# Three modulation vectors moved from TensorE's attention loop to VectorE, gates one job later

## The chip, the cores and the metric

The kernel runs on one core of a Trainium2 chip. It is one launch with a hand-written instruction stream for each engine: TensorE (PE, with PEld for its weight loads), VectorE (DVE), ScalarE (ACT), GpSimd (POOL) and SyncE (SP), which issues nearly all DMAs. The metric is the device time of one execution in microseconds; lower is better. The median of three runs before the change is 1446.85 us (1446.82 to 1449.01).

## The reference, cut to what matters

One layer of a hybrid diffusion block on 1024 latent tokens and 256 context tokens of 1024 features, all in float32. What the change touches is the modulation: six vectors of 1024 features made from one conditioning vector.

```python
def modulation(cond, w, b):            # w is ada_w, 1024 x 6144
    m = jax.nn.silu(cond) @ w + b
    return jnp.split(m, 6, axis=-1)
# h  = rmsnorm(x, g_mix_pre) * (1 + scale_1) + shift_1        vectors 1 and 0
# x1 = x + gate_1 * rmsnorm(mixer(h) @ w_out, g_mix_post)     vector 2
# h2 = rmsnorm(x1, g_ffn_pre) * (1 + scale_2) + shift_2       vectors 4 and 3
# y  = x1 + gate_2 * rmsnorm(swiglu(h2), g_ffn_post)          vector 5
```

The mixer is an input projection (1024 to 2816), then three groups of channels side by side: a long convolution by transforms, neighbourhood attention with 8 heads plus all context keys, and a gated linear recurrence (RG-LRU) that runs forward and backward. Then come the output projection, and a SwiGLU feed-forward of width 2816.

## The kernel before, in words

Features lie on partitions, tokens along the free dimension. A large float32 product is made of three passes: each weight tile and each input is split into a rounded head (`w_hi`, by ACT) and a rest (`w_lo`, by POOL), and TensorE sums head x head, head x rest and rest x head. One unit of this is called a job: 24 matmuls of up to 512 columns (`product` L1917 and following, `lat_job` L2078). The heads and rests of a job's weights are made while the job before it runs, from a double-buffered `raw` that SP loads (`raw_dma`, issue at L490; it waits until the rest of the weights two jobs back is made, since that frees the buffer).

The order on each engine is the order in which the code is written; semaphores tie the engines together. The stages are:

- Start (0 to about 114 us): filter tables, spectra, and modulation vectors 0 and 1 by TensorE (`mod_sums` L2017, `mod_columns` L2025, 16 column matmuls with the row of sums as the stationary tile).
- Input projection: 54 jobs (`JOBS`), from 114 to 445 us. The outputs are moved out of PSUM by DVE for even jobs and ACT for odd ones up to job 19 (`lat_out`), by ACT afterwards. Between jobs, TensorE runs the gates of the recurrence (`lru_gates` L2099; `GATES_AFTER` puts gates 0 to 3 behind jobs 6, 7, 11, 13), then transposes and transforms of the convolution. DVE does the short convolutions and scans of the recurrence (table `after`: behind job j it runs `after[j]`), then the convolution's stages. Gates 0 need `lru_conv(0)`, which DVE runs behind job 4.
- Attention: 32 units (4 head pairs x 8 blocks of queries), 453 to 606 us. TensorE's loop in step n is scores(n), turn(n-1), values(n-2). DVE adds the bias table and takes the minimum (L1723), ACT takes the exponential (L998), DVE normalises (L1733), TensorE transposes the probabilities (L2231, L2239), ACT copies them (L1010, L1012), TensorE multiplies by the values (L2254), and DVE copies the result (L1737). POOL makes the bias tables of the next head pair (L1211) and the rests of its keys (L1194). ACT makes the heads of the next keys in step 2 of each eight (`key_heads` L931).
- In each turn TensorE also makes one of the 32 chunks (128 features) of modulation vectors 2 to 5: 8 float32 matmuls with the conditioning vector as stationary tile (L2234, 16 instructions, since a float32 matmul is two), whose weights SP brought as `ada1` (512 KB per chunk); ACT copies the row of sums (L1011), and a matmul of one column in values() turns it into a column (L2248, two instructions).
- Output projection, then the feed-forward in two halves of 512 tokens: 22 tiles of two jobs (gate and up, `gu_tile`), and 24 down jobs. In a tile, DVE combines the two products (L1825, L1828) and makes the rest of the result (L1832); in tiles 5 to 12 of the first half DVE adds the mixer's residual behind it (L1773 and following). Tiles 13 to 21 hold nothing more.
- The end: the last down job, its square on ACT (L1105), the sum over features, a root, and four output rows of blocks written out.

## Time and profile before

| what | us |
|---|---|
| median of three runs | 1446.85 |
| the profiled execution | 1447.58 |
| its span, first to last instruction | 1445.8 |
| PE busy | 1403.6 (97%) |
| DVE busy | 744.8 (52%) |
| ACT busy | 552.8 (38%) |
| POOL busy | 612.9 (42%) |

The busy shares are means over stages with different limits, so a stage has to be read by itself: by the chain of work that ended last, by what an engine waited for in a stretch, and by the timeline of a few microseconds. Matmuls are pipelined, so a row's duration is longer than the distance to the next; distances are taken from start to start.

### The profile page before, as it was taken

Reading aid. Unit: us, or ns where it says so; the run is one execution under the profiler, and the core shown is the slowest. Engines: PE = TensorE matmul, PEld = TensorE weight load, DVE = VectorE, ACT = ScalarE, POOL = GpSimd, SP = SyncE. Lnnn points to the kernel's source line nnn. Section 1 sums busy time; section 2 is a strip of 40 time slices with the busy share of each in tenths; the row PEclk is TensorE's granted clock in tenths of the full one; section 3 lists DMA queues with packets and bytes.
Section 4 is the critical chain, followed back from the end, with each engine's and each line's share of the span. In section 5 each row is a group of like instructions: output and inputs, shape, how many; then the busy total and the mean of one; then the engine's idle time right before and its main releaser. Section 6 shows DMA issues by size and latency. Waiting matters only on the chain.

```text
span 1445.8 us, 20378 instructions
## 1 busy us (share of the span) xinstructions
PE 1403.6 (97%) x7745; PEld 1148.6 (79%) x7745; DVE 744.8 (52%) x1024; ACT 552.8 (38%) x863; POOL 612.9 (42%) x291
## 2 busy tenths in 40 slices
PE   5999999999998999999999999999999999999997
PEld 1589667899987888888788888888888888888885
DVE  7764557893945887447755541145456411110122
ACT  5662544321314777643432323332232223233222
POOL 3353122061435554383444444444444444444442
PEclk9999999999999999999999999999999999999999
DMA  9852111414213455443233333333333433332332
GB/s 328 319 168 70 48 44 29 131 30 131 59 30 101 137 139 151 147 143 105 74 101 88 94 98 99 94 95 99 94 98 97 136 102 101 94 95 85 94 100 85
DMA packets 236450, 156.67 MB, mean 108 GB/s; under 512 B 10531, under 2 KB 221873, under 8 KB 236251
## 3 DMA queue, kind: packets, MB, share of 16 engines
q1 hardware_dynamic: 234387, 148.70, 34.1%
q10 hardware_dynamic: 1992, 6.99, 1.3%
q8 instruction: 48, 0.79, 0.2%
q14 instruction: 23, 0.19, 0.0%
HBM read 147.25 MB, written 8.81 MB: 108 GB/s over the span
## 4 chain that ended last, share of the span: by engine, by line
PE 88%; DVE 5%; ACT 3%; issue 1%; DVEq 0%
PE ps L1923 36%; PE ps L1928 18%; PE ps L2091 11%; PE ps L2096 5%; PE ps L2254 2%; PE ps L2231 2%; PE ps L2192 2%; PE ps L2109 1%; PE ps L2150 1%; PE ps L2138 1%; PE ps L1985 1%; PE ps L1972 1%; PE ps L2234 1%; PE ps L1992 1%; ACT pr L998 1%
## 5 line engine op out<-in xcount | busy, mean ns | idle before, releaser
L1130 POOL TENSOR_TENSOR w_lo<-raw,w_hi 128x1024 fp32r<-128x1024 f32 x152 | 375.9, 2473 | 439.3 <-ACT w_hi L708 439.3
L1923 PE MATMUL ps<-hb_hi,w_hi 128*128 128x512 f32 x768 | 300.7, 392 | 1.6 <-DVE hb_lo L1790 1.6
L1923 PE MATMUL ps<-hb_lo,w_hi 128*128 128x512 f32 x768 | 298.9, 389 | 0.0
L708 ACT ACTIVATE w_hi<-raw 128x1024 fp32r<-128x1024 f32 x152 | 160.1, 1053 | 169.6 <-PE ps L1928 164.6
L1928 PE MATMUL ps<-hb_hi,w_lo 128*128 128x512 f32 x768 | 191.1, 391 | 0.0
L1150 POOL TENSOR_TENSOR w_lo<-raw,w_hi 128x1024 fp32r<-128x1024 f32 x21 | 88.6, 4219 | 222.2 <-ACT w_hi L862 222.2
L1923 PEld LDWEIGHTS ps<-hb_hi,w_hi 128*128 128x128 f32 x768 | 144.2, 188 | 33.2 <-DVE hb_lo L1790 3.4
L1928 PEld LDWEIGHTS ps<-hb_hi,w_lo 128*128 128x128 f32 x768 | 144.2, 188 | 31.2 <-issue 1.4
L1923 PEld LDWEIGHTS ps<-hb_lo,w_hi 128*128 128x128 f32 x768 | 144.2, 188 | 29.7 <-issue 0.2
L2091 PE MATMUL ps<-ha_hi,w_hi 128*128 128x512 f32 (+2 forms) x432 | 163.7, 379 | 3.1 <-ACT p_hy L869 2.8
L2091 PE MATMUL ps<-ha_lo,w_hi 128*128 128x512 f32 (+2 forms) x432 | 161.3, 373 | 0.0
L1923 PE MATMUL ps<-a_hi,w_hi 128*128 128x512 f32 x352 | 138.3, 393 | 0.0
L1923 PE MATMUL ps<-a_lo,w_hi 128*128 128x512 f32 x352 | 137.1, 389 | 0.0
L1828 DVE SCALAR_TENSOR_TENSOR a_f<-g_t,ps 128x512 f32<-128x512 f32 x44 | 30.2, 687 | 166.9 <-PE ps L1928 166.9
L1078 ACT ACTIVATE a_hi<-a_f 128x512 f32 (+1 forms) x44 | 27.8, 632 | 204.8 <-DVEq L1830 204.8
L2096 PE MATMUL ps<-ha_hi,w_lo 128*128 128x512 f32 (+2 forms) x432 | 99.1, 371 | 0.0
L2091 PEld LDWEIGHTS ps<-ha_hi,w_hi 128*128 128x128 f32 x432 | 81.7, 189 | 17.4 <-issue 3.2
L2091 PEld LDWEIGHTS ps<-ha_lo,w_hi 128*128 128x128 f32 x432 | 81.7, 189 | 10.4
L2096 PEld LDWEIGHTS ps<-ha_hi,w_lo 128*128 128x128 f32 x432 | 80.0, 188 | 10.3
L1928 PE MATMUL ps<-a_hi,w_lo 128*128 128x512 f32 x352 | 87.6, 389 | 0.0
L1825 DVE SCALAR_TENSOR_TENSOR g_t<-g_t,ps 128x512 f32<-128x512 f32 x44 | 30.2, 687 | 94.5 <-ACT g_t L1074 93.1
L1923 PEld LDWEIGHTS ps<-a_hi,w_hi 128*128 128x128 f32 x352 | 66.1, 188 | 13.8 <-issue 0.2
(293 smaller groups left out, 2104.6 us busy)
## 6 DMA issues: line engine op xcount, KB each, us to landing
raw<-in_ffn_w_gu SPq DMA_DIRECT2D x88, 512.0 KB, 3.8
ada1x<-in_ada_w SPq DMA_DIRECT2D x32, 512.0 KB, 4.0
raw<-in_ffn_w_down SPq DMA_DIRECT2D x32, 512.0 KB, 3.8
raw<-in_w_in SPq DMA_DIRECT2D x22, 512.0 KB, 3.9
ada<-in_ada_w SPq DMA_DIRECT2D x4, 2048.0 KB, 21.9
raw<-in_w_out SPq DMA_DIRECT2D x16, 512.0 KB, 3.9
raw<-in_ffn_w_down SPq DMA_DIRECT2D x16, 384.0 KB, 3.4
raw<-in_ktab SPq DMA_DIRECT2D x8, 512.0 KB, 5.5
```

Of the source, the lines that this page charges most:

```text
L708: act.activation(w_hi[:, b, :], raw[:, b, :], ACT.Copy).then_inc(hi_done, 1)
L1130: pool.tensor_tensor(w_lo[:, b, :], raw[:, b, :], w_hi[:, b, :].bitcast(F32), ALU.subtract).then_inc(lo_done, 1)
L1150: pool.tensor_tensor(w_lo[:, b, :], raw[:, b, :], w_hi[:, b, :].bitcast(F32), ALU.subtract).then_inc(llo, 1)
L1825: dve.scalar_tensor_tensor(g_t[:], g_t[:], 1.0, ps[:, 0, :], ALU.add, ALU.mult).then_inc(acc_free, 1)
L1828: dve.scalar_tensor_tensor(a_f[:], g_t[:], 0.5, ps[:, 1, :], ALU.mult, ALU.mult).then_inc(acc_free, 1)
L1923: pe.matmul(dst, w_hi[:, b, k * P:(k + 1) * P], x, start=start and i_ == 0 and n == 0, stop=False)
L1928: ins = pe.matmul(dst, w_lo[:, b, k * P:(k + 1) * P], rhs(k)[0], start=False, stop=stop and k == nk - 1)
L2091: pe.matmul(dst, w_hi[:, b, k * P:(k + 1) * P], x[:, k, a:z], start=k == 0 and n == 0, stop=False)
L2096: ins = pe.matmul(dst, w_lo[:, b, k * P:(k + 1) * P], ha_hi[:, k, a:z], start=False, stop=k == KT - 1)
L2192: ins = pe.matmul(dst, q_[hh, 4 * rb + cb, :], rhs, start=i == 0, stop=i == 2)
L2231: pe.transpose(ps[0:m, 4 + e, c * P:(c + 1) * P], pr[:, b, e, a:a + m], ident[:])
L2254: ins = pe.matmul(ps[hh, 7, 0:P], vtm[0:m, hp, tile, hh], pT[0:m, b, e, c, :], start=c == 0, stop=c == 4)
```

## The change

Modulation vectors 2 and 3 are made by DVE in the input projection. SP brings rows of `ada_w` in eight transfers of 1 MB, each holding two k-tiles of one vector (`rows_dma`; contiguous pieces of 4 KB), and DVE multiplies each k-tile by the conditioning value of its partition and adds it up (`modulation_rows`, two operations of 128x1024 per transfer). TensorE then sums over partitions with 16 matmuls of one column ahead of job 18, and DVE adds the bias (`modulation_columns`). Vector 5 is made in the same way in the first half of the feed-forward, one k-tile behind each of tiles 13 to 20, with eight transfers of 512 KB and 8 matmuls behind the last tile. Attention keeps the eight chunks of vector 4, in its last eight units. Gates 0 and 1 go behind jobs 7 and 8. At the end, the last square goes to the sum without DVE's addition, the last transposes stand behind the sum, and a square root of two numbers is put ahead of the second half's down jobs.

```diff
-GATES_AFTER = {6: 0, 7: 1, 11: 2, 13: 3}
+GATES_AFTER = {7: 0, 8: 1, 11: 2, 13: 3}
+ADA_UNIT = 24
+        adq = [p_hy[:, 2 * r:2 * r + 2, :] for r in range(2)]
+        adq_sum = [p_hy[:, 4 + v, :] for v in range(2)]
 # SP, input projection
+            def rows_dma(q):
+                if q >= 2:
+                    sp.wait_ge(mod_rd, 16 + q - 1)
+                else:
+                    sp.wait_ge(kjob, 8)
+                c, m = 2 * (q % 4), 2 + q // 4
+                sp.dma_start(adq[q % 2], ada[:, c:c + 2, m * D:(m + 1) * D]).then_inc(ada_ld[q % 2], 16)
+            rows_dma(0)
+            rows_dma(1)
             # (the 16 loads of l_w)
-            for fi in range(2, 4):
-                lat_raw(fi)
+            rows_dma(2)
+            rows_dma(3)
+            lat_raw(2)
+            lat_raw(3)
+            rows_dma(4)
+            rows_dma(5)
+            lat_raw(4)
+            lat_raw(5)
+            rows_dma(6)
+            rows_dma(7)
             sp.wait_ge(rz_ld, 16)
             sp.dma_start(rpad[:, 4:19, 8:39], A["na_rpb"][0]).then_inc(rp_ld, 16)
+            lat_raw(6)
+            lat_raw(7)
             # (the 16 issues of rskew)
-            for fi in range(4, 10):
-                lat_raw(fi)
+            lat_raw(8)
+            lat_raw(9)
 # SP, attention
-                chunk_dma(n)
+                if n >= ADA_UNIT + 2:
+                    chunk_dma(n - ADA_UNIT)
 # SP, feed-forward, first half (in place of the loop over tiles)
+                    def gate_rows(c):
+                        if c >= 2:
+                            sp.wait_ge(mod_rd, 32 + c - 1)
+                        else:
+                            sp.wait_ge(job_done, J_FFN)
+                        sp.dma_start(adf[c % 2][:], ada[:, c, 5 * D:6 * D]).then_inc(ada_ld[c % 2], 16)
+                    for i in range(1, FT):
+                        for b in range(2):
+                            raw_dma(b, J0 + 2 * i + b, src_g(i, b))
+                        if i == 5:
+                            gate_rows(0)
+                            gate_rows(1)
+                        if 14 <= i < 20:
+                            gate_rows(i - 12)
 # ACT
-                    act.activation(arow1[:, u % 2, :], ps[:, 6, 256:384], ACT.Copy)
+                    if u >= ADA_UNIT:
+                        act.activation(arow1[:, u % 2, :], ps[:, 6, 256:384], ACT.Copy)
+                    act.activation(arec[:, 0, :], ones[:, 0:2], ACT.Sqrt)     # ahead of the second half's down jobs
 # DVE
+            def modulation_rows(q):
+                dve.wait_ge(ada_ld[q % 2], 16 * (q // 2 + 1))
+                acc = adq_sum[q // 4]
+                for r in range(2):
+                    c = 2 * (q % 4) + r
+                    if c == 0:
+                        link(dve.tensor_scalar(acc, adq[q % 2][:, r, :], sil[:, 0, 0:1], None, ALU.mult))
+                    else:
+                        link(dve.scalar_tensor_tensor(acc, adq[q % 2][:, r, :], sil[:, 0, c:c + 1], acc, ALU.mult, ALU.add))
+                dve.nop().then_inc(mod_rd, 1)
+            def modulation_columns():
+                dve.wait_ge(mod_done, 19)
+                link(dve.tensor_tensor(mod[:, 16:32, 0], ps[:, 7, 0:16], colA[:, 64:80], ALU.add))
-            after = {4: lambda: lru_conv(0), 6: lambda: lru_conv(1),
+            after = {0: lambda: (modulation_rows(0), modulation_rows(1)), 2: lambda: (modulation_rows(2), modulation_rows(3)),
+                     4: lambda: lru_conv(0), 6: lambda: (lru_conv(1), *map(modulation_rows, range(4, 8))),
-                     18: lambda: (lru_input(3, 9), lru_backward(3), lru_join(3, 10)),
+                     18: lambda: (modulation_columns(), lru_input(3, 9), lru_backward(3), lru_join(3, 10)),
+                    for c in range(KT):                                       # feed-forward, first half
+                        gu_tile(13 + c)
+                        dve.wait_ge(ada_ld[c % 2], 16 * (c // 2 + 9))
+                        # tensor_scalar for c == 0, else scalar_tensor_tensor into adf_sum, as above
+                        dve.nop().then_inc(mod_rd, 1)
 # PE
+                if j == 18:
+                    pe.wait_ge(l_gate, 24)
+                    pe.wait_ge(mod_rd, 24)
+                    for m in range(2 * KT):
+                        ins = pe.matmul(ps[:, 7, m:m + 1], adq_sum[m // KT][:, (m % KT) * P:(m % KT + 1) * P], ones[:, 0:1],
+                                        start=True, stop=True)
+                    ins.then_inc(mod_done, 1)
+                if u >= ADA_UNIT:            # turn(u): the eight matmuls of a chunk; values(v): its column
+                    pe.wait_ge(ada_ld[b], 16 * ((u - ADA_UNIT) // 2 + 5))
 # (first half of the feed-forward, behind the last tile: 8 such column matmuls of adf_sum)
 # the end
-                    down_columns(KT - 1)
             pe.wait_ge(n_sum, 6)
-            for q in range(4):
-                ins = pe.matmul(ps[:, 0, q:q + 1], nrm[:, q * P:(q + 1) * P], ones[:, 0:1], start=True, stop=True)
+            for half in range(2):
+                for last in range(2):
+                    if last and half == 0:
+                        pe.wait_ge(y_sq, KT)
+                    for q in (2 * half, 2 * half + 1):
+                        src = sq[:, (KT - 1) % 2, q * P:(q + 1) * P] if last else nrm[:, q * P:(q + 1) * P]
+                        ins = pe.matmul(ps[:, q % 2, q // 2:q // 2 + 1], src, ones[:, 0:1], start=not last, stop=last == 1)
             ins.then_inc(n_ps, 1)
+            down_columns(KT - 1)
```

## Rows read from the trace of the kernel before

**Rows 1.** the page: the chain that ended last, shares by engine.

```profile
PE 88%; DVE 5%; ACT 3%; issue 1%; DVEq 0%
```

**Rows 2.** timeline of one attention turn, TensorE's weight loads (start, us, instructions).

```profile
524.62 0.86 PEld L2231 LDWEIGHTS ps<-ident,pr 128*128 128x128 f32 x8 [0.19 <-issue]
...
525.65 0.38 PEld L2234 LDWEIGHTS ps<-ada1x,silp 128*32 128x32 f32 x16 [0.17 <-issue]
526.22 0.20 PEld L2239 LDWEIGHTS ps<-ident,pr 128*128 128x128 f32 x2 [0.20 <-issue]
526.39 0.30 PEld L2248 LDWEIGHTS ps<-selc,arow 128*128 128x128 f32 x2
526.71 1.07 PEld L2254 LDWEIGHTS ps<-pT,vtm 96*64 96x64 f32 x20
...
529.02 0.86 PEld L2231 LDWEIGHTS ps<-ident,pr 128*128 128x128 f32 x8 [0.19 <-issue]
```

**Rows 3.** waits between engines from 483 to 570 us (total us, times, longest).

```profile
DVE pr L1723 <- PE ps L2192: 5.5, 11, 0.8
```

**Rows 4.** timeline of DVE and POOL in the same turns.

```profile
523.18 0.55 DVE L1733 TENSOR_SCALAR pr<-pr,arec 128x640 f32<-128x640 f32 x1
...
524.74 0.82 DVE L1723 CUSTOM_DVE_ANT_0 pr<-ps,tb 128x640 f32<-128x640 f32 x1 [0.78 <-PE ps L2192]
...
526.39 2.63 POOL L1211 TENSOR_TENSOR tb<-gt,mask 128x384 f32<-128x384 f32 x2 [5.84 <-DVE amin L1723]
...
526.76 1.18 DVE L1733 TENSOR_SCALAR pr<-pr,arec 128x640 f32<-128x640 f32 x1
...
529.49 0.81 DVE L1723 CUSTOM_DVE_ANT_0 pr<-ps,tb 128x640 f32<-128x640 f32 x1
```

**Rows 5.** timeline of DVE in the turn with the key heads.

```profile
509.42 0.17 DVE L1732 RECIPROCAL arec<-asum 128x1 f32<-128x1 f32 x1 [1.41 <-ACT pr L998]
```

**Rows 6.** timeline of TensorE: first gates, first channel transposes.

```profile
149.88 4.51 PE L2109 MATMUL ps<-l_u,l_w 64*64 64x256 f32 x24 [1.51 <-DVEq L1477]
...
256.53 1.12 PE L2122 MATMUL ps<-ident,conv 128*128 128x128 f32 x8 [1.57 <-DVEq L1528]
```

**Rows 7.** timeline of TensorE's weight loads at the start's column matmuls.

```profile
67.65 1.98 PEld L2025 LDWEIGHTS ps<-selc,arow 128*128 128x128 f32 x16
```

**Rows 8.** timeline of DVE and SP in the input projection; a transfer's row.

```profile
138.76 0.56 DVE L1461 TENSOR_SCALAR p_kv<-ps 128x384 f32<-128x384 f32 x1 [8.50 <-PE ps L2096]
...
170.23 0.69 DVE L1461 TENSOR_SCALAR p_xg<-ps 128x512 f32<-128x512 f32 x1 [13.72 <-PE ps L2096]
...
214.13 1.22 DVE L1514 SCALAR_TENSOR_TENSOR l_q<-l_q,p_xg 128x1024 f32<-128x1024 f32 x1
...
130.27 1.21 SPq L516 DMA_DIRECT2D raw<-in_w_in  x2
...
ada<-in_ada_w SPq DMA_DIRECT2D x4, 2048.0 KB, 21.9
```

**Rows 9.** the feed-forward: chain of TensorE, then DVE, POOL, SP, ACT.

```profile
845.29 3.63 PE ps L1923 x16
...
847.78 0.75 DVE L1773 SCALAR_TENSOR_TENSOR a_f<-yo,gmix,rstd 128x512 f32<-128x512 f32 x1 [0.16 <-DVE a_lo L1832]
...
847.92 2.87 POOL L1130 TENSOR_TENSOR w_lo<-raw,w_hi 128x1024 fp32r<-128x1024 f32 x1 [4.02 <-ACT w_hi L708]
...
1135.25 1.69 SPq L490 DMA_DIRECT2D raw<-in_ffn_w_gu  x2
...
1140.36 1.06 ACT L708 ACTIVATE w_hi<-raw 128x1024 fp32r<-128x1024 f32 x1 [2.53 <-DMA raw<-in_ffn_w_gu]
```

**Rows 10.** timeline of the end.

```profile
1434.44 0.69 DVE L1894 TENSOR_TENSOR nrm<-nrm,sq 128x512 f32<-128x512 f32 x1 [11.92 <-ACT sq L1105]
...
1435.43 0.97 PEld L2423 LDWEIGHTS ps<-ones,nrm 128*128 128x128 f32 x8
...
1436.52 0.16 DVE L1902 TENSOR_SCALAR var<-ps 128x4 f32<-128x4 f32 x1 [1.39 <-PE ps L2423]
```

More of the change, by code:

```diff
@@ L271, in program @@
         hb3_lo = at("hb3_lo", P_KV + 32768, [KT, HALF], F32R)
+        adf = [at("adf0", S_ + 32768, [D]), at("adf1", S_ + 36864, [D])]
+        adf_sum = at("adf_sum", S_ + 40960, [D])
         ysq = at("ysq", S_ + 2048, [HALF])
@@ L634, in chunk_dma @@
             def chunk_dma(n):
-                ada_dma(ada1, n % 2, 16 + n - 1 if n >= 2 else None, ada[:, :, (16 + n) * P:(17 + n) * P], ada_ld)
+                ada_dma(ada1, n % 2, 24 + n - 1 if n >= 2 else None, ada[:, :, (32 + n) * P:(33 + n) * P], ada_ld)
             sp.wait_ge(rs_ld, 256)
@@ L656, in _ @@
             sp.wait_ge(pv_done, 32)
-            sp.wait_ge(mod_done, 50)
+            sp.wait_ge(mod_done, 18 + 1 + 32 - ADA_UNIT)
             for q in range(4):
@@ L674, in _ @@
                 if h == 0:
-                    phase(J0, FT, src_g)
+                    def gate_rows(c):
[12 more added lines that the diff above has]
+                            gate_rows(i - 12)
                 else:
@@ L1740, in _ @@
             dve.tensor_tensor(hm_lo[5][:], mix_src(5, 0), hm_hi[5][:].bitcast(F32), ALU.subtract).then_inc(m_ld, 1)
-            dve.wait_ge(mod_done, 50)
-            link(dve.tensor_tensor(mod[:, 16:48, 0], ps[:, 7, 384:416], colA[:, 64:96], ALU.add))
+            dve.wait_ge(mod_done, 18 + 1 + 32 - ADA_UNIT)
+            link(dve.tensor_tensor(mod[:, 32:40, 0], ps[:, 7, 384 + ADA_UNIT:416], colA[:, 80:88], ALU.add))
             dve.nop().then_inc(modp, 1)
             link(dve.tensor_tensor(gmix[:], mod[:, 16:24, 0], colA[:, 24:32], ALU.mult))
-            link(dve.tensor_tensor(gffn[:], mod[:, 40:48, 0], colA[:, 40:48], ALU.mult))
             link(dve.scalar_tensor_tensor(affn[:], mod[:, 32:40, 0], 1.0, colA[:, 32:40], ALU.add, ALU.mult))
@@ L1858, in _ @@
                     dve.nop().then_inc(n_sum, 1)
+                    for c in range(KT):
+                        gu_tile(13 + c)
+                        dve.wait_ge(ada_ld[c % 2], 16 * (c // 2 + 9))
+                        if c == 0:
+                            link(dve.tensor_scalar(adf_sum[:], adf[0][:], sil[:, 0, 0:1], None, ALU.mult))
+                        else:
+                            link(dve.scalar_tensor_tensor(adf_sum[:], adf[c % 2][:], sil[:, 0, c:c + 1], adf_sum[:], ALU.mult, ALU.add))
+                        dve.nop().then_inc(mod_rd, 1)
                 else:
@@ L1875, in _ @@
                                         ps[:, 4 + 2 * (q % 2):6 + 2 * (q % 2), :].rearrange("p a b -> p (a b)")).then_inc(o_ev, 1)
-                i0 = 7 if h else 13
+                i0 = 7 if h else 21
                 with dve.Fori(i0, FT) as i:
@@ L1882, in _ @@
                 if h == 0:
+                    dve.wait_ge(mod_done, 28)
+                    link(dve.tensor_tensor(mod[:, 40:48, 0], ps[:, 7, 0:8], colA[:, 88:96], ALU.add))
+                    link(dve.tensor_tensor(gffn[:], mod[:, 40:48, 0], colA[:, 40:48], ALU.mult))
                     rstd_of(3)
@@ L1891, in _ @@
                 else:
-                    for k in range(1, KT):
+                    for k in range(1, KT - 1):
                         dve.wait_ge(y_sq, k + 1)
@@ L1901, in _ @@
             dve.wait_ge(n_ps, 6)
-            dve.tensor_scalar(var4[:], ps[:, 0, 0:4], 1.0 / D, EPS, ALU.mult, ALU.add).then_inc(n_var, 1)
+            dve.tensor_scalar(var4[:].rearrange("p (c b) -> p b c", b=2), ps[:, 0:2, 0:2], 1.0 / D, EPS, ALU.mult, ALU.add).then_inc(n_var, 1)
             for b in range(2):
@@ L1907, in _ @@
             link(dve.reciprocal(rstd4[:], var4[:]))
+            dve.wait_ge(t_tp, 4 + KT)
             for q in range(4):
@@ L2166, in _ @@
                     inverse(o, part, V_ROWS[o])
+                if j == 18:
[5 more added lines that the diff above has]
+                    ins.then_inc(mod_done, 1)
                 lat_job(j, (lambda: turn_channels(1)) if j == 22 else None)
                 if j in GATES_AFTER:
-                    if j == 6:
+                    if j == 7:
                         pe.wait_ge(lw_ld, 256)
@@ L2231, in turn @@
                         pe.transpose(ps[0:m, 4 + e, c * P:(c + 1) * P], pr[:, b, e, a:a + m], ident[:])
-                pe.wait_ge(ada_ld[b], 16 * (u // 2 + 1))
-                for k in range(KT):
-                    ins = pe.matmul(ps[32 * (k % 4):32 * (k % 4) + 32, 6, 256:384], silp[:, k, :],
-                                    ada1[:, b, k * P:(k + 1) * P], start=k < 4, stop=k >= 4)
-                ins.then_inc(mod_rd, 1)
+                if u >= ADA_UNIT:
+                    pe.wait_ge(ada_ld[b], 16 * ((u - ADA_UNIT) // 2 + 5))
+                    for k in range(KT):
+                        ins = pe.matmul(ps[32 * (k % 4):32 * (k % 4) + 32, 6, 256:384], silp[:, k, :],
+                                        ada1[:, b, k * P:(k + 1) * P], start=k < 4, stop=k >= 4)
+                    ins.then_inc(mod_rd, 1)
                 a, m = chunks[4]
@@ L2247, in values @@
                     pe.wait_ge(ot_free, v)
-                pe.matmul(ps[:, 7, 384 + v:385 + v], arow1[:, b, :], selc[:, 0:1], start=True, stop=True).then_inc(mod_done, 1)
+                if v >= ADA_UNIT:
+                    pe.matmul(ps[:, 7, 384 + v:385 + v], arow1[:, b, :], selc[:, 0:1], start=True, stop=True).then_inc(mod_done, 1)
                 for c in range(5):
@@ L2373, in _ @@
                 if h == 0:
+                    pe.wait_ge(mod_rd, 40)
+                    for m in range(KT):
+                        ins = pe.matmul(ps[:, 7, m:m + 1], adf_sum[:, m * P:(m + 1) * P], ones[:, 0:1], start=True, stop=True)
+                    ins.then_inc(mod_done, 1)
                     sum_over_features(3, nrm)
```

## Prediction

> **What bounds the kernel now.** Start with the chain that ended last: 88% of it is TensorE [rows 1], so an instruction taken from TensorE is worth its distance, unless another engine sets the pace at that place. The removed work lies in attention, so read one turn there next. From one turn's transposes to the next turn's it is 529.02 - 524.62 = 4.40 us [rows 2]. Of these, the chunk takes 526.22 - 525.65 = 0.57 us and its column 526.71 - 526.39 = 0.32 us: 0.89 us per turn. TensorE alone would so give 24 x 0.89 = 21.4 us. But is TensorE what each turn waits for? The waits of the stretch with the 20 steps 6 to 25 say how long DVE's first operation of a step waited for the scores: 5.5 us, in 11 of the 20 [rows 3]. The other nine started without a wait. DVE and POOL show why: normalising takes 0.55 us where POOL is idle and 1.18 us under POOL's bias table; after that one, the next step of DVE starts at 529.49 with no wait in front of it, 4.75 us after the last, while the step before had 0.78 us to spare [rows 4]. So in this stretch DVE, slowed by POOL, is nearly as late as TensorE. What TensorE saves comes back only up to DVE's waits.
>
> **Attention, what is removed.** In steps 6 to 25 the gain is the 5.5 us that DVE waited [rows 3]. Steps 0 to 5 overlap POOL throughout; I give them nothing. In the step with the key heads DVE waits 1.41 us for ACT [rows 5], and ACT loses one small copy there; in three such steps I take 0.5 us for the three together (it lies between 0 and their 4.2 us of waits, and the copy is the smallest of what ACT does there). Steps 26 to 31 keep their chunks and gain nothing. Sum: -6.0 us. Ends: 0 us if DVE and ACT set every step and the 5.5 us reappear elsewhere, -21.4 us if TensorE set every step. I stay at 6.0, since a wait is a ceiling for what its releaser can give. After the change TensorE should need 4.40 - 0.89 = 3.51 us for a step and DVE without POOL 4.40 - 0.78 = 3.62 us, so DVE is the later one in all of them.
>
> **Gates one job later.** Today TensorE waits 1.51 us for the short convolution ahead of the first gates [rows 6]. A job lies between afterwards, 24 matmuls at 3.63/16 us = 5.4 us [rows 9], so the wait goes: -1.5 us. What comes later instead is gates 0 on ACT and the recurrence behind them; DVE next needs them behind job 8, where it idles 13.72 us [rows 8]. Ends: -1.5 and +1 us.
>
> **What DVE does instead.** An operation of 128x1024 with two inputs in SBUF takes 1.22 us [rows 8]. Four of them behind job 0 (about 5 us) and four behind job 2 stand against idle stretches of 8.50 us at job 4, and one like it at job 2; eight behind job 6 (10 us with the gaps) stand against 13.72 us [rows 8]. They come free in time if their transfers do. Transfers 0 and 1 are issued as soon as the last spectrum is stored, while DVE is busy with other work. Transfers 2 and 3 (2 MB) are issued behind the 16 small loads of the gates' weights, and the raw weights of job 6 now stand behind them in SP's queue. Four transfers of 2 MB in flight together took 21.9 us [rows 8], 2.7 us per MB, so 2 MB delay the weights by at most 5.5 us. Today they are issued at 130.27 [rows 8]; with 0.7 us for two more issues, 5.5 us and the 5.1 us that weights took behind another transfer [rows 9], they land at 141.6 at the latest. Job 6 ends at 149.88 - 1.51 = 148.4 today and so starts at 143.0; ACT's head takes 1.06 us [rows 9] and must begin by 141.9. I take 0 us, with 3 us as the other end. Transfers 6 and 7 wait for DVE's own progress, land some 4 us later, and push the eight operations to about 13 us, near the whole idle stretch; a POOL operation in the way adds 2.4 us. TensorE needs the bank that DVE frees behind them only when gates 1 (4.51 us) and job 9 (5.4 us) are done, 10 us after job 8. I take 0, with +3 us as the other end.
>
> **Columns.** The 16 matmuls of one column ahead of job 18 are 32 instructions. At the start, 16 such instructions took 1.98 us of weight loads [rows 7], at the end 8 took 0.97 [rows 10]: 0.12 us each, 3.8 us. Nothing hides them, since TensorE waits for no one at job 18, and the chain of DVE that it waits for later (1.57 us at the first channel transposes [rows 6]) begins behind job 18 and moves with it. DVE's bias addition stands ahead of that chain: +0.2 us. The eight in the feed-forward are 16 instructions: +1.9 us. Ends for all: 4 to 7 us.
>
> **The feed-forward's first half.** DVE is idle most of a tile, so the one operation behind each of tiles 13 to 20 costs it nothing. The queue to watch is SP's. From tile 14 to 19, SP waits for DVE's operation behind the tile before, and the raw weights of the next tile's first job stand behind this wait. Count from job start 845.29, which is the end of a tile [rows 9]. Work like DVE's new operation starts at 847.78 today, 0.14 us ahead of POOL, and is not slowed; POOL is (2.87 us) [rows 9]. The new one, of 1.22 us, ends at 849.0, and SP goes on at about 849.3: the row transfer, then the raw weights at about 849.7. Elsewhere in this trace SP issued weights right behind another transfer at 1135.25, and ACT could start on them at 1140.36, 5.1 us later [rows 9]. So ACT starts at 854.8 and is done at 855.9; the job that needs them starts two jobs after 845.29, at 856.2. The slack is 0.3 us: I take 0, and name the rest as a rival.
>
> **The end.** Today DVE's last addition (from 1434.44) and the wait of the sum behind four transposes put the variance at 1436.52 [rows 10]. Afterwards 12 of the 16 small instructions follow the square, which is ready at about 1434.4: 12 x 0.12 = 1.45 us, so variance at about 1436.0: -0.5 us (ends 0 and -0.8). The square root put ahead costs ACT time where it has a job in hand: 0.
>
> **Sum.** -6.0 - 1.5 + 0 + 3.8 + 0.2 + 1.9 + 0 - 0.5 = -2.1 us. The profiled execution took 1447.58 us (span 1445.8 and 1.8 around it) and would take 1445.5; it stands 0.7 us above the median of 1446.85, so the median comes to 1444.8 us.
>
> **Rivals.**
> - *SP's queue in the feed-forward* (slower). The 0.3 us of slack are used up if POOL takes its turn first: then DVE's operation ends near 850.8 + 1.2 = 852.0 rather than 849.0, ACT has the weights 3.0 us later, and TensorE waits 2.7 us in each of six tiles: +16 us, 1461 us. If SP or the transfer is only 1 us slower than counted it is 6 x 0.7 = +4 us, 1449 us. It decides from 0.3 us of delay on. For it: the 0.14 us between DVE and POOL. Against it: in the row shown DVE came first, with the same instructions ahead of it.
>   The Trainium skill, page "SBUF — State Buffer", section "SBUF: two separate sides", says that a DVE operation with two SBUF inputs and a GpSimd operation that reads SBUF hold their port in turn, and that the one that starts second fully blocks. The trace agrees as to order: POOL, starting second, took 2.87 us. By that rule this rival is all or nothing per tile.
> - *TensorE's pace in attention* (faster). POOL's tables start when DVE has finished with the old ones; if shorter turns let more of them fall beside operations that aren't slowed, the nine unwaited steps shorten too. Each slow pair costs 2 x (1.18 - 0.55) = 1.3 us [rows 4]; half of nine gone is 6 us more: 1439 us. Against it: the table starts at 526.39 because DVE finished its minimum just before, so they stay tied.
> - *The projection's queue* (slower). Row transfers land late, DVE is still on them when job 8's or job 4's bank should come free, or job 6's weights come late: +3 to +6 us, 1448 to 1451 us. For it: 0.3 us of room for the weights of job 6 by the upper bound.
> - *Attention gives nothing*: DVE's waits were only reordered, and the columns' 5.9 us stay: 1446.85 - 1.5 + 5.9 - 0.5, 1450.7 us. For it: nine of 20 steps of DVE wait for nothing. Against: 11 do.
>
> **Chances.** 0.2% of the time is 2.9 us, what a measurement can tell from no change: faster is below 1444.0, slower above 1449.7. Forecast 0.50 (own range 1442.5 to 1447; 0.13 of it below 1444.0). TensorE's pace 0.18, all faster. SP's queue 0.15 (0.10 slower, 0.05 within). Projection's queue 0.10 (0.05 slower). Attention gives nothing 0.07 (0.05 slower). Together faster 0.31, same 0.49, slower 0.20. The range for 8 in 10 is 1440 to 1450.5.
>
> **What would show it.** Attention: starts of L1723 in steps 6 to 25 without waits for scores, and the same steps about 5.5 us shorter together; L1733 still near 1.2 us under L1211. No wait ahead of the first L2109. The weight loads ahead of job 18 within 4 us. L708 in tiles 15 to 20 starting at most 0.3 us before it would make L1923 wait; a wait of L1923 for `w_hi` there shows the first rival. No new wait of L2091 for `lfree` or `w_hi` from job 4 to job 10. The prediction is wrong if attention shortens by less than 3 or more than 9 us, or if TensorE gains a wait over 1 us anywhere else.

## The result, and the profile after

| | us |
|---|---|
| kernel before, median of 4 runs beside it | 1447.93 (1446.82 to 1449.02) |
| changed kernel, median of 4 runs | 1459.47 (1459.03 to 1459.72) |
| ratio, 95% interval | 1.008, 1.0068 to 1.0091 |
| profiled execution, span before and after | 1445.8 and 1457.6 |

The change makes the kernel 11.5 us slower. Forecast were 1444.8 us and a range up to 1450.5 us. The forecast failed in one place above all, and a table by stage finds it. Each line is the start of the same instruction in both traces, subtracted; the first column says what the prediction had for the stage.

| stage | predicted | measured |
|---|---|---|
| start to job 6 of the projections | 0 | -0.9 |
| job 6 to job 17 (gates one job later) | -1.5 | -1.2 |
| job 17 to the start of job 18 (16 columns) | +3.8 | +3.8 |
| job 18 to job 22 (bias added by DVE, and more) | +0.2 | +2.9 |
| rest of the projections | 0 | 0.0 |
| attention up to the output projection | -6.0 | -6.0 |
| output projection, feed-forward to tile 15 | 0 | 0.0 |
| tiles 15 to 21 of the feed-forward's first half | 0 | +12.0 |
| tile 21 to the first down job (8 columns) | +1.9 | +1.8 |
| the end | -0.5 | -0.5 |

The sum of the measured column is +11.9, the two spans differ by 11.85. The first line is no effect of the change: among the ten profiled executions below job 0 starts anywhere from 111.2 to 115.5 us, also in kernels that differ only much later. All comparisons by trace are therefore made over distances inside a run. In this table they run between starts of TensorE's matmuls.

Start with the page of the changed kernel, its chain by engine, which answers to [rows 1]: TensorE's share fell from 88% to 77%, and DMA and SP's queue stand in it for the first time.

```profile
PE 77%; DVE 10%; ACT 4%; issue 2%; DMA 2%; SPq 1%; DVEq 0%; ACTq 0%
```

Next, who waits between 860 and 940 us (engine line waited for: us in total, times, longest):

```profile
ACT w_hi L751 <- DMA raw<-in_ffn_w_gu: 28.6, 6, 6.0
...
PE ps L1996 <- ACT w_hi L751: 7.4, 5, 2.4
```

TensorE waits for the rounded weights, ACT for the raw ones. The timeline from the first row operation to the first late matmul, five engines in order of time (start, us, engine, instructions, in brackets the idle time ahead); tile 15 starts at 865.53:

```profile
857.30 0.75 DVE L1925 TENSOR_SCALAR adf_sum<-adf,sil 128x1024 f32<-128x1024 f32 x1
857.45 2.86 POOL L1175 TENSOR_TENSOR w_lo<-raw,w_hi 128x1024 fp32r<-128x1024 f32 x1 [4.02 <-ACT w_hi L751]
...
858.14 0.34 SPq L709 DMA_DIRECT2D adf<-in_ada_w  x1
858.52 2.18 SPq L495 DMA_DIRECT2D raw<-in_ffn_w_gu  x2
...
864.10 1.06 ACT L751 ACTIVATE w_hi<-raw 128x1024 fp32r<-128x1024 f32 x1 [3.22 <-DMA raw<-in_ffn_w_gu]
...
865.24 2.40 POOL L1175 TENSOR_TENSOR w_lo<-raw,w_hi 128x1024 fp32r<-128x1024 f32 x1 [4.93 <-ACT w_hi L751]
...
865.53 0.39 PE L1996 MATMUL ps<-hb_hi,w_hi 128*128 128x512 f32 x1
...
867.34 0.86 DVE L1894 TENSOR_TENSOR a_lo<-a_f,a_hi 128x512 fp32r<-128x512 f32 x1 [0.85 <-ACT a_hi L1122]
...
868.34 2.40 POOL L1175 TENSOR_TENSOR w_lo<-raw,w_hi 128x1024 fp32r<-128x1024 f32 x1 [0.69 <-ACT w_hi L751]
868.35 3.47 DVE L1927 SCALAR_TENSOR_TENSOR adf_sum<-adf,sil,adf_sum 128x1024 f32<-128x1024 f32 x1 [0.16 <-DVE a_lo L1894]
...
871.90 0.34 SPq L709 DMA_DIRECT2D adf<-in_ada_w  x1
872.29 1.06 SPq L495 DMA_DIRECT2D raw<-in_ffn_w_gu  x2
...
877.47 1.06 ACT L751 ACTIVATE w_hi<-raw 128x1024 fp32r<-128x1024 f32 x1 [5.71 <-DMA raw<-in_ffn_w_gu]
...
878.67 0.47 PE L1996 MATMUL ps<-hb_hi,w_hi 128*128 128x512 f32 x1 [2.11 <-ACT w_hi L751]
```

Read it from the top. At the first row operation DVE is 0.15 us ahead of POOL, as in [rows 9], and ends at 858.05; SP goes on, and the raw weights it issues at 858.52 reach ACT at 864.10, 5.6 us later, not the 5.1 us counted. That is in time for TensorE, but ACT has stood 3.2 us for them, so POOL's operation starts at 865.24, 0.3 us ahead of tile 15, instead of 3.6 us ahead of it. It still runs when DVE starts the operation ahead of the row operation (L1894, two SBUF inputs), which takes 0.86 us instead of 0.69 us. So the row operation starts 2.82 us behind the tile's start instead of 2.67 us, and POOL's next operation, which stands where it always did, 2.81 us behind the tile's start, is 0.01 us ahead of it. The row operation is held: it takes 3.47 us, 2.2 us more than the 1.28 us that it takes undisturbed, and ends 1.1 us behind POOL's. SP waits for it, the weights are issued at 872.29, and TensorE stands for 2.1 us. From the next tile on the late weights bring POOL 0.7 to 0.8 us ahead of the row operation, and each tile repeats it: five tiles, +2.3, +2.7, +2.2, +2.6 and +2.1 us.

In two of the five TensorE hardly stands (0.3 and 0.2 us) and works at a lower clock instead; these slices lie in tiles 17 and 19 (start and end, length, busy time of TensorE, of its weight loads, of DVE, ACT and POOL, then the granted clock, 1.00 being full speed, and two values of the DMA engines):

```profile
890.00:894.00 4.00, 1.76 (x4) 1.49 (x5) 1.99 (x2) 2.64 (x3) 1.82 (x1) 0.77 0.48 117
894.00:898.00 4.00, 4.00 (x15) 3.16 (x14) 3.84 (x2) 0.00 (x0) 3.37 (x2) 0.80 0.00 0
918.00:922.00 4.00, 3.21 (x9) 2.57 (x10) 2.65 (x2) 2.22 (x3) 3.28 (x2) 0.68 0.07 18
```

The clock is not what makes them long: there too the next tile's first matmul starts 0.14 us behind the end of ACT's head, as it does at 877.47 + 1.06 + 0.14 = 878.67, so the weights set the time.

The other unforeseen size stands behind the columns. TensorE's weight loads there, then the mean granted clock in slices of 4 us (the third value from the end of a line):

```profile
230.39 4.42 PEld L2244 LDWEIGHTS ps<-ones,p_hy 128*128 128x128 f32 x32
234.69 0.33 PEld L2164 LDWEIGHTS ps<-ha_hi,w_hi 128*128 128x128 f32 x1
...
235.34 0.33 PEld L2164 LDWEIGHTS ps<-ha_hi,w_hi 128*128 128x128 f32 x1
235.76 0.33 PEld L2164 LDWEIGHTS ps<-ha_lo,w_hi 128*128 128x128 f32 x1
```

```profile
226.00:230.00 4.00, 4.00 (x18) 3.27 (x17) 3.97 (x2) 0.98 (x1) 2.37 (x1) 0.93 0.08 20
230.00:234.00 4.00, 4.00 (x33) 3.88 (x31) 1.05 (x1) 1.54 (x2) 1.57 (x1) 0.92 0.39 115
234.00:238.00 4.00, 4.00 (x13) 3.32 (x13) 0.00 (x0) 0.00 (x0) 0.79 (x1) 0.50 0.44 128
238.00:242.00 4.00, 4.00 (x15) 3.19 (x14) 0.00 (x0) 0.00 (x0) 0.00 (x0) 0.72 0.01 3
```

From the first of the 32 loads to the first of job 18 it is 4.3 us; job 17 is 0.3 us shorter than before, so the stage is 3.8 us longer by the starts of the matmuls, as foreseen. But behind them the clock is at its lower level, 1.2 GHz: loads of job 18 stand 0.42 us apart instead of 0.23 us, though no row shows TensorE idle. That is most of the +2.9 us; 0.2 us of them are the bias addition.

The gates start without a wait where [rows 6] had 1.51 us, here TensorE's row:

```profile
152.80 4.51 PE L2182 MATMUL ps<-l_u,l_w 64*64 64x256 f32 x24
```

With the gates alone this makes job 6 to job 10 1.6 us shorter. Here it gives less, 1.2 us to job 17: from job 9 to job 11 TensorE takes 0.4 us more than in that kernel, and job 10 starts behind a wait of 0.15 us for DVE's move out of PSUM (L1506). Of the nine traced kernels with DVE's row operations in the projections six have this delay and three do not; what decides it was not looked into.

In attention, 483 to 570 us as in [rows 3], the waits of DVE for scores are gone, and one of TensorE for ACT is there instead, 10.3 us in total where the kernel before had 1.5 us:

```profile
PE ps L2311 <- ACT pT L1056: 10.3, 15, 1.4
```

And at the end the variance starts 2.2 us behind the last product instead of 2.7 us [rows 10]; here DVE's row:

```profile
1448.38 0.16 DVE L1974 TENSOR_SCALAR var<-ps 128x4 f32<-128x4 f32 x1 [13.48 <-PE ps L2513]
```

### The profile page after: what moved, and what is told of

Same layout as the page of the kernel before. It is cut to its first block, busy times and chain, and to the rows that moved or that the text cites. A ratio compares the mean times of both kernels' runs of the same rounds, so it can differ in the third digit from the quotient of the medians.

```text
span 1457.6 us, 19409 instructions
## 1 busy us (share of the span) xinstructions
PE 1398.7 (96%) x7369; PEld 1144.1 (78%) x7369; DVE 799.2 (55%) x1049; ACT 549.5 (38%) x840; POOL 615.7 (42%) x291
## 4 chain that ended last, share of the span: by engine, by line
PE 77%; DVE 10%; ACT 4%; issue 2%; DMA 2%; SPq 1%; DVEq 0%; ACTq 0%
PE ps L1996 34%; PE ps L2001 17%; PE ps L2164 9%; PE ps L2169 4%; ACT pr L1041 2%; DMA raw<-in_ffn_w_gu 1%; DVE pr L1796 1%; DVE pr L1786 1%; PE ps L2223 1%; PE ps L2211 1%; PE ps L2058 1%; DVE p_hy L1733 1%; PE ps L2045 1%; DVE adf_sum L1927 1%; PE ps L2065 1%
## 5 line engine op out<-in xcount | busy, mean ns | idle before, releaser
L1118 ACT ACTIVATE g_t<-ps 128x512 f32<-128x512 f32 x44 | 26.3, 598 | 136.3 <-PE ps L2001 136.3
```

Of the source, the lines that this page charges most:

```text
L1118: act.activation(g_t[:], ps[:, 0, :], ACT.Tanh, scale=0.5).then_inc(g_tanh, 1)
```

## The experiments

Ten kernels in three groups; each group has its own runs of the kernel before, and the ratios are against those.

| kernel | us, median | before beside it | ratio, 95% interval |
|---|---|---|---|
| rows one tile later | 1447.74 | 1447.24 | 1.0001, 0.9988 to 1.0014 |
| the same, columns ahead of job 17 | 1444.96 | 1447.24 | 0.9981, 0.9969 to 0.9993 |
| the same, columns spread | 1441.94 | 1447.24 | 0.9959, 0.9943 to 0.9975 |
| projections' part only | 1446.95 | 1447.24 | 0.9997, 0.9986 to 1.0008 |
| row operation with one input | 1456.90 | 1447.65 | 1.0054, 1.0041 to 1.0067 |
| row operation on half the columns | 1455.97 | 1447.65 | 1.0039, 1.0020 to 1.0058 |
| 16 columns alone | 1454.66 | 1447.65 | 1.0045, 1.0032 to 1.0057 |
| gates alone | 1447.22 | 1447.65 | 0.9997, 0.9988 to 1.0005 |
| row operation with its sum in PSUM | 1449.79 | 1447.31 | 1.0011, 0.9998 to 1.0024 |
| rows one tile later, operation in two parts | 1447.31 | 1447.31 | 0.9997, 0.9988 to 1.0006 |

### Rows one tile later

```
-                        if 14 <= i < 20:
-                            gate_rows(i - 12)
+                        if 15 <= i < 21:
+                            gate_rows(i - 13)
```

> Only the order in SP's queue changes: the row transfers 2 to 7 of the feed-forward stand one tile later (tiles 15 to 20), so SP waits for an operation of DVE that was done a tile before; the transfers, DVE's operations and their tiles are the same. Theory A (the wait in SP's queue holds back the raw weights of the next tile): the five tiles that took 2.4 us each too long lose it, -12 us against the changed kernel, 1447.5 us, and no wait of TensorE over 1 us for w_hi between tiles 14 and 20. Rival B (the six transfers of 512 KB themselves slow the weights): they still run beside the weights, so most of the 12 us stays, 1457 to 1459.5 us. Rival C (DVE's operation blocked by POOL, 3.2 to 3.5 us rather than 1.22 us, delays DVE's own work): it is still there, so 1457 to 1459.5 us.

The six row transfers are the same, but they are issued 3.0 us or more ahead of the next weights, not 0.4 us.

Measured: 1447.74 us, 11.7 us less than the changed kernel. In its trace tiles 15 to 21 take exactly as long as before the change (the difference to the kernel before stays at -4.56 us from tile 5 to tile 21). DVE and POOL of one tile:

```profile
864.13 0.69 DVE L1894 TENSOR_TENSOR a_lo<-a_f,a_hi 128x512 fp32r<-128x512 f32 x1 [0.84 <-ACT a_hi L1122]
864.99 1.28 DVE L1927 SCALAR_TENSOR_TENSOR adf_sum<-adf,sil,adf_sum 128x1024 f32<-128x1024 f32 x1 [0.16 <-DVE a_lo L1894]
...
865.13 3.40 POOL L1175 TENSOR_TENSOR w_lo<-raw,w_hi 128x1024 fp32r<-128x1024 f32 x1 [4.03 <-ACT w_hi L751]
```

All seven two-input row operations take 1.28 us, and POOL, coming 0.14 us later, takes 3.40 us. So the same operations and as many transfers cost nothing once SP's wait is one tile older: theory A. B is settled only as far as the transfers stand in this order; the kernel with the sum in PSUM, further down, keeps each right ahead of the weights and bounds it. C is not tested here, since DVE isn't held at all.

### How much is the hold, how much the way from SP to ACT

Three kernels leave every wait and transfer of the changed kernel in place and alter only DVE's row operation in the feed-forward. Each leaves something out of the gate vector, so their results are not the layer's: the running sum, half of the columns, or the true sum (what happens to be in PSUM is read in its place).

```
# cut: ".." stands for arguments left out
-  scalar_tensor_tensor(adf_sum[:], adf[c % 2][:], sil[..], adf_sum[:], ALU.mult, ALU.add)
+  tensor_scalar(adf_sum[:], adf[c % 2][:], sil[..], None, ALU.mult)          # one input
+  scalar_tensor_tensor(adf_sum[:, 0:HALF], adf[c % 2][:, 0:HALF], ..)        # half the columns
+  scalar_tensor_tensor(adf_sum[:], adf[c % 2][:], sil[..], ps[:, 4:6, :], ..)  # sum from PSUM
```

> The changed kernel as it is, with SP's waits in their places, but DVE's row operation of the feed-forward has one input in SBUF (a row times its scalar, nothing added, so the gate vector is wrong): 0.75 us instead of 1.28 us. Theory P (a DVE operation with two SBUF inputs that starts 0.01 us behind POOL is held until POOL is done, and that 2.2 us is what TensorE waits in each tile): with one input DVE isn't held, the operation stays at 0.75 us though POOL is in the same place, and at least 10 of the 12 us go: 1447.5 us. Rival L (the way from SP's issue to ACT, 5.6 us rather than the 5.1 us counted, is what makes each tile late, and the port only adds DVE time that nobody waits for): the operation ends 0.5 us earlier only, so at most 0.5 us a tile goes, 1456 to 1457 us.

> The changed kernel as it is, but DVE's row operations behind tiles 14 to 20 work on 512 of the 1024 columns (the gate vector is wrong in the other half): two inputs in SBUF, about 0.7 us, as short as the operation with one input. Theory P: it is held behind POOL like the full one whenever POOL starts first, 2.4 + 0.7 = 3.1 us instead of 3.47 us, so TensorE still waits some 2 us a tile: 1456 to 1457.5 us. Rival L (length of the operation, not the port): like the operation with one input, whatever that gives; if that one loses the 12 us, so does this one, 1447.5 us.

> The changed kernel as it is, all waits and transfers in their places, but the running sum that DVE's row operation adds to is read from PSUM instead of SBUF (so the gate vector is wrong): one SBUF input, no mode of double rate, about 1.3 us as before. DVE's operations of 128x512 with a PSUM input stayed at 0.69 us under POOL in the changed kernel's trace, so this one should not be held. Theory P (the hold behind POOL is what keeps TensorE waiting 2.4 us in each tile): 10 to 12 us go, 1447.5 to 1449.5 us, with at most 0.5 us a tile left of the way from SP to ACT. Rival L (that way alone, 5.6 us, makes the tiles late): the operation's length and SP's order are unchanged, so 1457 to 1459.5 us.

Measured with one input: 1456.90 us. Theory P's number is missed and L's is met, but the trace says why, and it isn't L's reason. POOL, then DVE:

```profile
869.27 2.39 POOL L1175 TENSOR_TENSOR w_lo<-raw,w_hi 128x1024 fp32r<-128x1024 f32 x1 [0.66 <-ACT w_hi L751]
...
869.31 2.90 DVE L1927 TENSOR_SCALAR adf_sum<-adf,sil 128x1024 f32<-128x1024 f32 x1
```

The operation with one SBUF input is held too: 2.90 us instead of 0.75 us, and tiles 15 to 21 still lose 9.2 us. What I had wrong was which operations are held, not whether the hold matters. The rows of before had shown it: L1733, a TENSOR_SCALAR with one tensor input, took 0.55 us with POOL idle and 1.18 us beside it [rows 4]. The Trainium skill, page "SBUF — State Buffer", section "SBUF: two separate sides", names a DVE operation in a mode that uses two ports beside the one with two SBUF inputs. The run agrees with it as far as it goes: this form does 1024 columns in 0.75 us where the one with two inputs takes 1.28 us, which looks like such a mode, and it was held for 2.15 us. The number of inputs alone does not explain the shorter time: with its second input in PSUM the operation takes 1.28 us as well (below).

Measured with half the columns: 1455.97 us, 0.03 us under P's range; held, 2.95 us instead of 0.75 us, and tiles 15 to 21 lose 9.4 us. Here are POOL and DVE:

```profile
868.04 2.40 POOL L1175 TENSOR_TENSOR w_lo<-raw,w_hi 128x1024 fp32r<-128x1024 f32 x1 [0.70 <-ACT w_hi L751]
...
868.04 2.95 DVE L1927 SCALAR_TENSOR_TENSOR adf_sum<-adf,sil,adf_sum 128x512 f32<-128x512 f32 x1 [0.16 <-DVE a_lo L1894]
```

Its twelve runs lie between 1444.78 and 1459.01 us, wider than any other's. Two of them are as fast as a kernel without the stall and three more lie near 1451 us; whether the chain of late tiles started later or not at all in those is not known, since the one execution with a trace (1457.23 us) has it.

Measured with the sum in PSUM: 1449.79 us, 0.3 us above P's range and 7.2 us below L's. The timeline has the same order as the changed kernel, POOL first by 0.03 us, but DVE's operation is not held:

```profile
870.52 2.40 POOL L1175 TENSOR_TENSOR w_lo<-raw,w_hi 128x1024 fp32r<-128x1024 f32 x1 [0.68 <-ACT w_hi L751]
...
870.55 1.28 DVE L1927 SCALAR_TENSOR_TENSOR adf_sum<-adf,sil,ps 128x1024 f32<-128x1024 f32 x1 [0.16 <-DVE a_lo L1894]
...
872.30 1.06 SPq L495 DMA_DIRECT2D raw<-in_ffn_w_gu  x2
...
877.62 1.06 ACT L751 ACTIVATE w_hi<-raw 128x1024 fp32r<-128x1024 f32 x1 [3.67 <-DMA raw<-in_ffn_w_gu]
...
890.41 0.47 PE L1997 MATMUL ps<-hb_hi,w_hi 128*128 128x512 f32 x1 [0.46 <-ACT w_hi L751]
```

Length, waits and transfers are those of the changed kernel, and tiles 15 to 21 cost 2.4 us instead of 12.0 us (0.1 to 0.7 us a tile). So 9.6 us of the 12.0 us are the hold of the row operation, shown by taking it away.

The 2.4 us that stay are in part the way over SP to ACT: from SP's issue it takes 5.1 to 5.7 us in these tiles, where the count had 5.1 us. Another part is a hold again: L1894, ahead of the row operation, takes 0.87 us in tile 15 and 1.3 to 1.7 us in the next five instead of 0.69 us, so the row operation starts 2.8 to 3.05 us behind the tile's start instead of 2.67 us. How much is each was not measured. The 2.4 us are also the most that the six transfers can cost by themselves.

And there was no slack for either. The count took 845.29 as the tile's start, which is a time of the chain; the matmul itself starts earlier, and the next tile's starts 10.88 us later, at 856.00. Here is TensorE's row of the kernel before:

```profile
845.12 0.39 PE L1923 MATMUL ps<-hb_hi,w_hi 128*128 128x512 f32 x1
```

In each late tile the first matmul starts 0.14 us behind the end of ACT's head. The count's 855.9 and 0.14 us make 856.0: the slack was nil, not 0.3 us.

### A hold that nobody waits for

```
+  for a, z in ((0, 256), (256, D)):      # on top of "rows one tile later"
+      scalar_tensor_tensor(adf_sum[:, a:z], adf[c % 2][:, a:z], .., adf_sum[:, a:z], ..)
```

> The kernel with the rows one tile later, and DVE's row operation in two parts of 256 and 768 columns, so that POOL, which was 0.14 us behind, gets its turn between them and the second part is held. The result is the same. Theory A (a held DVE operation costs only through what waits for it, and SP no longer waits for this one in the same tile): the second part takes 3 us or more and the time stays 1447.5 us. Rival C (the hold itself makes DVE's own work late): the second part ends before DVE's next operation is due in both cases by 0.3 us or less, so up to 1 us a tile, 1450 to 1453 us.

Measured: 1447.31 us. DVE's two parts together and POOL's operation that gets in between:

```profile
864.82 3.55 DVE L1928 SCALAR_TENSOR_TENSOR adf_sum<-adf,sil,adf_sum 128x256 f32<-128x256 f32 x2 [0.16 <-DVE a_lo L1894]
...
864.97 2.59 POOL L1175 TENSOR_TENSOR w_lo<-raw,w_hi 128x1024 fp32r<-128x1024 f32 x1 [4.03 <-ACT w_hi L751]
...
868.52 0.69 DVE L1887 SCALAR_TENSOR_TENSOR g_t<-g_t,ps 128x512 f32<-128x512 f32 x1 [0.15 <-ACT g_t L1118]
```

The hold is there in each of the seven tiles: the second part takes 3.03 us. DVE's next operation (L1887) starts 0.09 us later behind the tile's start than in the kernel without the split (6.36 and 6.27 us), and the tiles take as long as before the change. The hold by itself costs nothing (theory A); it costs only through SP's queue.

### The columns

16 matmuls of one column alone, added to the kernel before ahead of job 18:

```
+  if j == 18:
+      pe.wait_ge(l_gate, 24)
+      for m in range(2 * KT):
+          pe.matmul(ps[:, 7, m:m + 1], ident[:], ones[:, 0:1], start=True, stop=True)
```

> The kernel before with nothing but 16 matmuls of one column ahead of job 18 (the results are not used). Theory A (32 small instructions of 0.12 us, and a half-clock stretch of the granted clock behind them): +3.8 us for the instructions and +2.9 us for the clock, 1453.9 us against 1447.2 us. Rival B (the clock drop has to do with the row operations or transfers of the changed kernel): +3.8 us, 1451.0 us.

Measured: 1454.66 us, 7.0 us above the kernel before, where A said 6.7 us. Its slices of the granted clock:

```profile
230.00:234.00 4.00, 4.00 (x33) 3.80 (x31) 2.82 (x1) 1.54 (x2) 1.22 (x2) 1.00 0.46 131
234.00:238.00 4.00, 4.00 (x14) 3.42 (x14) 0.00 (x0) 0.00 (x0) 1.26 (x1) 0.51 0.33 98
238.00:242.00 4.00, 4.00 (x13) 3.11 (x13) 0.00 (x0) 0.00 (x0) 0.00 (x0) 0.64 0.11 33
```

The clock falls behind the small instructions without any row operation or row transfer. The median meets A's number partly by chance. By the trace the projections lose 5.2 us: 3.8 + 2.8 us less 1.4 us, because the lower stretch that the kernel before has in job 17 is missing in this run. Another 1.2 us stand at the start of the feed-forward, where the clock is lower for a short stretch (two kernels without these columns, the gates alone and the projections' part only, have such a stretch too), and 1.0 us is spread over attention and the second half.

Ahead of job 17, and spread, both on top of "rows one tile later":

```
-                if j == 18:
+                if j == 17:                              # all 16 ahead of job 17
+                if 17 <= j <= 20:                        # or four ahead of each
+                    for m in range(4 * (j - 17), 4 * (j - 17) + 4):
```

The spread kernel has a second edit: with its last columns ahead of job 20, DVE's bias addition moves from behind job 18 into the convolution's stage, behind the first short convolution.

> As the run with the rows one tile later, and the 16 matmuls of one column stand ahead of job 17, not 18, in a stretch where TensorE waits 2.8 us for lat_out. Theory A (the 32 small instructions cost 3.8 us only because nothing covers them, and the drop of the granted clock behind them costs another 2.9 us): 2.8 us less than that run, 1444.7 us, and 5.6 us less, 1441.9 us, if the clock stays up because the same idle time is now filled. Rival B (the place does not matter, the wait of job 17 moves on behind the columns): no change, 1447.5 us.

> As the run with the rows one tile later, and the 16 matmuls of one column are spread, four ahead of each of jobs 17 to 20. Theory A (32 small instructions in one row are what the granted clock falls behind): no half-clock stretch at jobs 18 to 20, which gives back 2.9 us, and one eighth to one quarter of the instructions falls into the wait of job 17: -2.9 to -3.8 us against that run, 1443.7 to 1444.6 us. Rival B (the drop comes from somewhere else, the clock falls at about 233 us anyhow): -1 us or less, 1446.5 to 1447.5 us.

Measured: 1444.96 us and 1441.94 us, against 1447.74 us with all columns ahead of job 18. The first is A's number for a clock that still falls, the second lies 1.8 us below A's range; B is out in both. The start alone differs by up to 4 us between executions, so the trace gives the better size: from job 16 to the end of the projections the kernels lose 5.4 us (ahead of 18), 0.7 us (ahead of 17) and 0.8 us (spread) against the kernel before. Ahead of job 17 the columns fill the wait of 2.8 us for ACT, which is gone. The clock falls behind them there too, to 0.62 in the slice from 222 to 226 us, but the kernel before has such a stretch in job 17 anyway (0.66 from 226 to 230 us), so it costs little more. Spread, eight instructions stand in that wait and the others never come in a long row; the slices of that kernel:

```profile
226.00:230.00 4.00, 4.00 (x17) 3.22 (x17) 3.97 (x2) 1.12 (x2) 2.52 (x1) 0.89 0.04 13
230.00:234.00 4.00, 4.00 (x23) 3.44 (x22) 1.21 (x1) 1.55 (x2) 1.32 (x1) 1.00 0.40 118
234.00:238.00 4.00, 4.00 (x24) 3.41 (x22) 0.55 (x1) 0.00 (x0) 1.08 (x1) 1.00 0.42 120
238.00:242.00 4.00, 4.00 (x19) 3.32 (x19) 3.93 (x4) 0.00 (x0) 0.00 (x0) 1.00 0.04 12
```

None of these slices behind 230 us is below full clock, though eight column instructions stand ahead of each of jobs 18, 19 and 20. The spread saves something else besides: the first channel transposes had waited 1.8 us for DVE, and now TensorE gets there without a wait:

```profile
255.48 1.05 PE L2197 MATMUL ps<-ident,conv 128*128 128x128 f32 x8
```

Of the 4.6 us between all ahead of job 18 and spread (5.4 and 0.8 us), this is 1.8 us; the spread is therefore no measure of the clock by itself. The two kernels differ by 3.0 us in their medians but by 0.1 us in this stage, and their profiled spans are 1438.6 us (ahead of 17) and 1439.5 us (spread), so which is better isn't settled. By the medians both beat the kernel before, the spread one by 5.3 us, and both intervals leave out 1.

### Parts by themselves

```
-GATES_AFTER = {6: 0, 7: 1, 11: 2, 13: 3}       # gates alone
+GATES_AFTER = {7: 0, 8: 1, 11: 2, 13: 3}
-                    if j == 6:
+                    if j == 7:
```

> The kernel before with nothing but the first two gates one job later. Theory A (the wait of 1.51 us ahead of the first gates goes, and nothing else is late): job 10 starts 1.2 to 1.5 us earlier, 1445.9 us. Rival B (the gates' results come later on ACT and a wait for them takes the place of the old one before job 18): 0, 1447.2 us.

Measured: 1447.22 us, 0.4 us under the kernel before, which a measurement can't tell from nothing. In the trace job 6 to job 10 is 1.6 us shorter, and at the end of attention 1.4 us of it are still there; a lower stretch of the clock between 700 and 710 us takes 1.5 us back. The mechanism is shown, a gain in time isn't.

```
+ADA_UNIT = 16      # two vectors by DVE; attention keeps 16 of 24 chunks; the feed-forward's part undone
```

> The feed-forward's part is undone: only the two vectors of the projections are made by DVE, and attention keeps 16 of its 24 chunks. Theory A (the feed-forward's part costs 12 us of late weights and 1.8 us of columns, and eight chunks fewer in attention give about a third of 6.0 us): 1459.5 - 13.8 + 2 = 1447.7 us. Rival B (what the chunks of attention give does not go by their number, since DVE is the later engine as soon as some are gone): with 16 removed it gives the full 6 us, 1445.7 us; if it gives nothing until all are gone, 1451.7 us.

Measured: 1446.95 us, 0.75 us below A and 1.25 us above B's first number, which the median alone can't tell apart. The trace does: from the end of the projections to the output projection 4.4 us are gained with 16 chunks removed, 6.0 us with 24. A had 4 us, B the full 6 us or nothing.

## Why the prediction was wrong

**The feed-forward's first half** is the step that failed. It said: "The slack is 0.3 us: I take 0, and name the rest as a rival." Measured are +12.0 us, and the runs with the rows one tile later and with the sum in PSUM show where from. Two things in it were wrong. First there was no slack: the count began 0.17 us behind the tile's first matmul and left out the 0.14 us from ACT's head to the matmul, and the way from SP to ACT, read from a single row, is up to 0.6 us longer than 5.1 us. Second, and that is 9.6 us, the order of DVE and POOL was read from [rows 9] and taken to hold in every tile: "in the row shown DVE came first, with the same instructions ahead of it". The weights that stand behind SP's first wait reach ACT 3.3 us later than before, still in time for TensorE; but the POOL operation that follows them then overlaps DVE's operation ahead of the row operation and holds it for 0.17 us. That is more than DVE's lead of 0.14 us. POOL's place in the tile had not moved; DVE's had.

**The first rival**, SP's queue, was the right mechanism: order, place and hold. Its price was 2.7 us in six tiles, 16 us; it came to 2.4 us in five, since SP's first wait is for the operation with one input, which DVE starts 0.15 us ahead of POOL. At a chance of 0.15 it was undervalued: a slack of 0.3 us behind a way of 5.1 us read from one row, in a loop where one late tile makes the next one late, is no step at 0. That the right mechanism was named is to the prediction's credit; the sum did not use it.

**Columns.** The 3.8 us for 32 instructions and the 1.9 us for 16 were right (3.8 and 1.8). Missed were 2.7 us (2.9 less the 0.2 us of the bias) for the lower clock behind the 32; no row of before showed such a series inside running work, and the bound of 7 us for all was left by 1.5 us.

**Attention.** The sum of -6.0 us was right, and nearly its split: by the starts of the minimum (L1723, after the change L1786) steps 6 to 25 brought 4.9 us for the 5.5 us and steps 0 to 5, which were given nothing, 1.2 us. That the two misses cancel is luck. DVE's waits for scores went as foreseen, but ACT, not DVE, is what TensorE waits for now. With 16 of 24 chunks removed 4.4 of the 6.0 us are there, about in proportion.

**Gates**: -1.6 us alone, for -1.5 us. **DVE's rows in the projections**: +0.4 us at jobs 9 and 10 for 0, within the end of +3 us; this is what makes the gates' -1.6 us the -1.2 us of the table. Three of the nine traced kernels with these operations do not have it. **Bias**: the wait at the first channel transposes went from 1.57 to 1.77 us, +0.2 us as forecast. **The end**: -0.5 us as forecast.

The rest of the sum stands. The forecast of -2.1 us with the 2.7 us of the clock gives +0.6 us; the kernel with the rows one tile later measured +0.5 us. With the columns at 0.8 us in place of 4.0 us the forecast gives -5.3 us; the spread kernel measured -5.3 us (1441.94 for 1447.24). The intervals are some 2 us wide to either side, so the agreement to 0.1 us is partly luck.

## What to carry to other kernels

A wait put into the queue that issues weights has to be priced with everything that stands behind it, and its slack computed from one kind of mark throughout and with the other engines where the change puts them, not where the old trace shows them; when the slack is a few tenths of a us and the place is in a loop, wait for something one turn older. Of a DVE operation that others wait for, ask whether it can be held by POOL; reading one operand from PSUM or giving it nobody who waits makes the hold harmless. Here a long row of tiny matmuls cost more than its own time: spread it, or put it where TensorE stands anyway.

## What the runs showed of the hardware

- A hold of DVE behind POOL: 1.28 us became 3.47 us with POOL 0.01 us ahead; with one SBUF input 0.75 us became 2.90 us; with one operand in PSUM and POOL 0.03 us ahead it stayed at 1.28 us. A DVE operation of 128x512 with two SBUF inputs (L1894) went from 0.69 us to as much as 2.48 us behind POOL. With DVE 0.14 us ahead it is POOL that takes longer, 3.40 us for 2.39 us.
- Behind 32 back-to-back instructions of one-column matmuls TensorE's granted clock was at 0.50 to 0.51 for a slice of 4 us and at 0.64 to 0.72 for the next, in three kernels (the changed one, rows one tile later, columns alone), with and without the row operations, though TensorE was busy throughout; behind rows of 8 such instructions ahead of jobs 18, 19 and 20 it stayed at 1.00.
- A transfer of 512 KB issued 0.4 us behind another took 5.1 to 5.7 us from SP's issue to ACT's start; the single row of before had 5.1 us.
